# Carry matrices of a chunked recurrence built in one run of products, and two pairs of product loops interleaved

## The reference, cut to what matters

```
def step(S, inp):                      # S: 8 heads x 64 x 64, one step for each of 256 tokens
    r_t, w_t, k_t, v_t, kk_t, a_t = inp
    s_kk = einsum("bhvk,bhk->bhv", S, kk_t)
    S = S * w_t - s_kk[..., None] * (kk_t * a_t)[:, :, None, :] + v_t[..., None] * k_t[:, :, None, :]
    return S, einsum("bhvk,bhk->bhv", S, r_t)
```

## Time and profile before

| what | value |
|---|---|
| median of 3 runs | 1668.27 us (1666.89 to 1669.16) |
| profiled execution, its own time | 1668.85 us |
| its span | 1667.0 us |
| PE busy | 1591.9 us, 95% of the span |
| DVE, ACT, POOL busy | 1136.0, 838.3, 108.4 us |
| mean granted clock of PE | 0.98 of full speed |

### The profile page before, as it was taken

The page is one execution under the profiler, slowest core; times in us unless marked ns, Lnnn a source line. Parts: engine busy times, 40 slices in busy tenths (PEclk is TensorE's granted clock), DMA queues, the critical chain, the costliest instruction groups (busy, mean ns, idle before and its releaser), DMA issues.

```text
span 1667.0 us, 26114 instructions
## 1 busy us (share of the span) xinstructions
PE 1591.9 (95%) x10308; PEld 1388.3 (83%) x10308; DVE 1136.0 (68%) x1415; ACT 838.3 (50%) x1267; POOL 108.4 (7%) x145
## 2 busy tenths in 40 slices
PE   6888899989999999999899999999999999999999
PEld 6777789978888888887788888888889987788887
DVE  4775485558767777675767767766678956667675
ACT  6553255554444644454754444644457657654443
POOL 0258000000000000000000000000000015100000
PEclk9899899999999999999999999999999999999999
DMA  6230025335555454545335454555444541355553
GB/s 259 103 126 2 2 102 189 127 139 196 180 197 178 154 201 176 199 158 177 127 127 202 176 201 177 179 176 201 177 175 153 186 171 74 102 177 192 186 189 113
DMA packets 37075, 263.60 MB, mean 158 GB/s; under 512 B 4224, under 2 KB 4352, under 8 KB 5760
## 3 DMA queue, kind: packets, MB, share of 16 engines
q1 hardware_dynamic: 35712, 257.97, 43.5%
q0 software_dynamic: 704, 2.62, 0.4%
q10 hardware_dynamic: 576, 1.84, 0.3%
HBM read 261.36 MB, written 1.05 MB: 157 GB/s over the span
## 4 chain that ended last, share of the span: by engine, by line
PE 86%; DVE 8%; ACT 5%; issue 1%; DMA 1%; SPq 0%; DVEq 0%; ACTq 0%
PE PS L539 21%; PE PS L469 14%; PE PS L471 13%; PE PS L470 13%; PE PS L540 10%; PE PS L543 3%; PE PS L743 2%; PE PS L542 1%; DVE w_lo L1732 1%; ACT w_hi L1186 1%; PE PS L437 1%; DMA raw_weights<-W 1%; DVE arena L2032 1%; PE PS L553 1%; PE PS L757 1%
## 5 line engine op out<-in xcount | busy, mean ns | idle before, releaser
L1732 DVE TENSOR_TENSOR w_lo<-raw_weights,w_hi 128x1024 fp32r<-128x1024 f32 x488 | 592.9, 1232 | 367.5 <-ACT w_hi L1186 366.8
L1186 ACT ACTIVATE w_hi<-raw_weights 128x1024 fp32r<-128x1024 f32 x488 | 505.8, 1054 | 291.8 <-PE PS L471 141.4
L539 PE MATMUL PS<-h_both,w_hi 128*128 128x512 f32 x1470 | 527.5, 398 | 0.0
L540 PE MATMUL PS<-h_both,w_lo 128*128 128x256 f32 x1470 | 412.5, 281 | 0.0
L539 PEld LDWEIGHTS PS<-h_both,w_hi 128*128 128x128 f32 x1470 | 276.6, 188 | 59.0
L540 PEld LDWEIGHTS PS<-h_both,w_lo 128*128 128x128 f32 x1470 | 277.7, 189 | 8.7
L469 PE MATMUL PS<-h_both,w_hi 128*128 128x256 f32 x560 | 162.6, 290 | 10.1 <-DVE w_lo L1732 7.1
L469 PE MATMUL PS<-w_hi,g_hi 128*128 128x512 f32 x440 | 171.5, 390 | 0.0
L471 PE MATMUL PS<-w_hi,g_lo 128*128 128x512 f32 x440 | 171.2, 389 | 0.0
L470 PE MATMUL PS<-w_lo,g_hi 128*128 128x512 f32 x440 | 171.2, 389 | 0.0
L470 PE MATMUL PS<-h_both,w_hi 128*128 128x256 f32 x560 | 160.7, 287 | 0.0
(11 more groups left out here) (410 smaller groups left out, 1995.0 us busy)
## 6 DMA issues: line engine op xcount, KB each, us to landing
raw_weights<-W SPq DMA_DIRECT2D x244, 1024.0 KB, 4.8
post_gain<-post_gains POOLq DMA_DIRECT2D x3, 512.0 KB, 3.7
x_resid<-x SPq DMA_DIRECT2D x2, 512.0 KB, 6.9
arena<-mem POOLq DMA_DIRECT2D x1, 1024.0 KB, 5.3
out<-x_resid SPq DMA_DIRECT2D x2, 512.0 KB, 2.6
ptab<-cols ACTq DMA_DIRECT2D x1, 857.0 KB, 8.9
ctab<-consts ACTq DMA_DIRECT2D x1, 758.0 KB, 5.9
rtab<-rows ACTq DMA_DIRECT2D x1, 176.0 KB, 12.0
```

Source lines behind the costliest of these rows:

```text
L539: mm(both_out, hi, h_both[:, :, c, :], start=c == 0, stop=False)
L540: mm(PS[:, bank + j, 0:T], lo, h_hi[:, c, :], start=False, stop=False)
L1186: A(w_hi[:, n % H, :], raw[:, n % (2 * R), :], ACT.Copy).then_inc(S.hi_ready, 1)
L1732: v.tensor_tensor(w_lo[:, n % H, :], raw[:, n % (2 * R), :], w_hi[:, n % H, :].bitcast(F32), ALU.subtract).then_inc(S.lo_ready, 1)
```

## The change

`state_bu` and `rows_carried` take a list of chunks and alternate between them inside the loop over the four 128-column slices. `carry` becomes `carries`, which writes the identity of both carry matrices first, each as one product of 512 columns (the identity repeated four times by a broadcast view), and then the eight products of the two matrices in turn, chunk 1 (rows 64 to 127, bank 2) and chunk 2 (rows 0 to 63, bank 0). The calls move accordingly: chunk 1's `state_bu` goes ahead of the carries and is alternated with chunk 0's; chunk 2's carry moves ahead of `state_kv(1)` and `state_bu(2)`; PE waits for the second XA copy before both carries; `rows_carried(2)` waits for the last `z_ready` and alternates with `rows_carried(3)`. No instruction of another engine is changed.

```
-            def state_bu(g):
+            def state_bu(gs):
                 for c, cs in enumerate(pairs):
-                    last = mm(PS[:, 4 + g, cs], B_t[half(g), g // 2, cs], U0[half(g), g // 2, cs], start=False,
-                              stop=g == 0 and c == 3)
-                if g == 0:
-                    last.then_inc(S.z_done, 1)
+                    for g in gs:
+                        last = mm(PS[:, 4 + g, cs], B_t[half(g), g // 2, cs], U0[half(g), g // 2, cs], start=False,
+                                  stop=g == 0 and c == 3)
+                        if g == 0 and c == 3:
+                            last.then_inc(S.z_done, 1)
-            def carry(g, bank):
+            def carries():
+                banks = (2, 0)
+                for bank in banks:
+                    mm(PS[:, bank, :].rearrange("p (c d) -> p c d", c=4), ident_r,
+                       ident_r.unsqueeze(1).broadcast_to([P, 4, P]), start=True, stop=False)
                 for c, cs in enumerate(pairs):
-                    mm(PS[:, bank, cs], ident_r, ident_r, start=True, stop=False)
-                    last = mm(PS[:, bank, cs], XA[half(g), g // 2, cs], B_t[half(g), g // 2, cs], start=False, stop=True)
-                last.then_inc(S.gt_done, 1)
+                    for g, bank in zip((1, 2), banks):
+                        last = mm(PS[:, bank, cs], XA[half(g), g // 2, cs], B_t[half(g), g // 2, cs], start=False,
+                                  stop=c == 3)
+                        if c == 3:
+                            last.then_inc(S.gt_done, 1)
-            def rows_carried(g):
-                t, cp = g // 2, 64 * (g % 2)
+            def rows_carried(gs):
                 for c, cs in enumerate(pairs):
-                    last = mm(PS[cp:cp + 64, Y_BANK[g], cs], RT[...], Zs[g - 1][:, c, :], start=False, stop=c == 3)
-                last.then_inc(S.yc_done, 1)
+                    for g in gs:
+                        t, cp = g // 2, 64 * (g % 2)
+                        last = mm(PS[cp:cp + 64, Y_BANK[g], cs], RT[...], Zs[g - 1][:, c, :], start=False, stop=c == 3)
+                        if c == 3:
+                            last.then_inc(S.yc_done, 1)
             state_kv(0)
             ...
-            state_bu(0)
-            pe.wait_ge(S.xa_ready, 1)
-            carry(1, 2)
-            state_bu(1)
+            state_bu((0, 1))
+            pe.wait_ge(S.xa_ready, 2)
+            carries()
             pe.wait_ge(S.convY_ready, 4)
             state_kv(1)
             pe.wait_ge(S.u_ready, 2)
-            state_bu(2)
-            pe.wait_ge(S.xa_ready, 2)
-            carry(2, 0)
+            state_bu((2,))
             pe.wait_ge(S.gt_ready, 1)
             ...
             rows_own(1)
-            rows_carried(2)
             pe.wait_ge(S.z_ready, 3)
-            rows_carried(3)
+            rows_carried((2, 3))
```

More of the change, by code:

```diff
@@ L867, in rows_own @@
                                 last.then_inc(S.yc_done, 1)
-            def rows_carried(g):
-                t, cp = g // 2, 64 * (g % 2)
+            def rows_carried(gs):
                 for c, cs in enumerate(pairs):
-                    last = mm(PS[cp:cp + 64, Y_BANK[g], cs], RT[:, t * 512 + c * P + cp:t * 512 + c * P + cp + 64],
-                              Zs[g - 1][:, c, :], start=False, stop=c == 3)
-                last.then_inc(S.yc_done, 1)
+                    for g in gs:
+                        t, cp = g // 2, 64 * (g % 2)
+                        last = mm(PS[cp:cp + 64, Y_BANK[g], cs], RT[:, t * 512 + c * P + cp:t * 512 + c * P + cp + 64],
+                                  Zs[g - 1][:, c, :], start=False, stop=c == 3)
+                        if c == 3:
+                            last.then_inc(S.yc_done, 1)
             state_kv(0)
@@ L895, in _ @@
             pe.wait_ge(S.rt_ready, 1)
-            rows_carried(1)
+            rows_carried((1,))
             state_gz(2)
```

## The result

The changed kernel takes 1657.64 us (median of 4 runs, 1655.65 to 1659.30) against 1668.20 for the kernel before, run beside it: ratio 0.9935, 95% interval 0.9923 to 0.9948. That is 10.6 us faster (8.7 to 12.8 by the interval), where 8.2 to 8.7 were forecast (1660.0 against the median of the kernel before, 1660.1 against its profiled execution). The time lies inside the range of 1657 to 1666, 0.6 us above its lower end. The profiled execution took 1655.98 us, with a span of 1654.2.

What follows compares the result with a forecast made beforehand. PE's own work, in the order of products the change rewrites, was taken as the bound. Some 4.0 us from order and 4.7 from half clock sum to 8.7, giving 1660.0 us, range 1657.0 to 1666.0.

Steps and rivals of the forecast that it cites:

- 1. state_bu of chunks 0 and 1: Sixteen alternating instructions in place of eight take 0.98 us, the same as chunk 0's alone; chunk 1's own eight vanish.
- 2. wait for the second XA copy: PE's wait moves ahead of both carries; price 0, cover 2.0 us, at most 0.69 us were the copy late.
- 3. both carries: Two wide identities and one change of shape, 0.66 us, then sixteen alternating instructions, 1.00; sum 1.66, bounds 1.3 to 2.9.
- 4. state_kv(1), state_bu(2): Products behind the carries, chunk 2 alone in state_bu, all in one row half: 1.87 us, waits covered.
- 5. reads: 64 instructions of 64 x 64 in all four array quarters: 1.0 us at full clock, against 1.91 at half clock.
- 6. state_gz(1): Behind reads: 1.08 us at full clock like its twin state_gz(2), against 1.60 mostly at half clock.
- 7. rows_own, rows_carried(1), state_gz(2): Products behind state_gz(1), unchanged at 6.14 us; the moved z_ready wait keeps 0.8 us of cover.
- 8. last products to projection: Alternated rows_carried of chunks 2 and 3, then ACT evacuations: 2.39 us stays, price 0; without overlap 0.66 us lost.
- no fall of the clock: PE's clock stays at 1.00 throughout the stretch, with one-row-half products of 1.87 us left; chance 0.68.
- rival of the late evacuation: Pairing rows_carried of chunks 2 and 3 delays chunk 2's ACT evacuation by 0.66 us, to 1660.8; chance 0.04.
- the one of missing overlap: In carries the row halves don't overlap, or the repeated view is slow: 1.2 us more, 1661.3; chance 0.08.
- half clock of 4.7 us: Gain from full clock: 1.9 second carry, 1.3 the 2.72 us before it, 0.9 reads, 0.5 state_gz(1).

Runs made afterwards that it cites:

- run 7: Changed kernel with output products of chunks 2 and 3 one after the other, the last z_ready wait between them; median 1658.62 us, ratio 0.9940 to the kernel before.
- run 5: Changed kernel without alternating: state_bu and, behind both wide identities, carry products one chunk after the other; median 1662.23 us, ratio 0.9960 to the kernel before.
- run 3: Changed kernel with sliced carries again, a 128-column identity product ahead of each slice's product; median 1667.58 us, ratio 1.0002 to the kernel before.
- Run 4: Kernel before with one edit: each carry writes its identity as one 512-column product, order and halves as before; median 1659.12 us, ratio 0.9952.
- run 6: Changed kernel with each wide identity as four of 128 columns, all eight ahead of the carry products; median 1660.18 us, ratio 0.9951 to the kernel before.
- run 8: Changed kernel with 24 extra 64-row products, all in row half 0, just ahead of reads; median 1663.37 us, ratio 0.9967 to the kernel before.
- run 10: Changed kernel with eight extra pairs of a 128-row and a 64-row float32 product just ahead of reads; median 1664.18 us, ratio 0.9976 to the kernel before.

## Why the prediction was right

Step by step against the profile after, in us:

| step | forecast | measured |
|---|---|---|
| 1. state_bu of chunks 0 and 1 | 0.98 | 0.99 |
| 2. wait for the second XA copy | 0 | 0 |
| 3. both carries | 1.66 | 1.66 |
| 4. state_kv(1), state_bu(2) | 1.87 | 1.88 |
| 5. reads | 1.0 | 1.09 |
| 6. state_gz(1) | 1.08 | 1.09 |
| 7. rows_own, rows_carried(1), state_gz(2) | 6.14 | 6.14 |
| 8. last products to projection | 2.39 | 2.39 |
| whole stretch's gain | 8.7 | 8.59 |

Each duration was taken from a row of the kernel before in which the same shapes ran in the same pattern: `carries` was priced by state_kv(0), reads by L736 at full clock. That no fall of the clock would come was right too, and so were the waits that were to stay covered. The rival of the late evacuation is refuted by run 7, the one of missing overlap by run 5 and the table. The prediction named a rule of the Trainium skill ("TensorE: Matmul & The Clock Gate", The mechanism) that spoke for the late evacuation: a weight load overlaps products in flight only where the row group differs. This trace disagrees. The chunks of L882 share all 128 rows and differ in columns, and the sixteen products take 1.10 us alternated (1.59 in turn) with PE busy all through, while their weight loads take 0.86 of it:

```profile
207.22 0.86 PEld L882 LDWEIGHTS PS<-arena 128*64 128x64 f32 x16
```

Two things were off. The size: 10.6 and 10.0 us were measured, not 8.2 to 8.7, and the forecast time of 1660.0 lies 2.4 us above the median. The steps at full clock came out as forecast. The term that was too small is the half clock of 4.7 us, read from one profile in which it lasted 10.24 us; in the second profile of the same kernel it lasted 13.65, and the stretch was 27.39 us, 1.54 longer, a gain of 10.1 by the stretch. What lies outside the stretch moves from one execution to the next: it took 1636.9 to 1641.2 us in the fourteen profiles, 1641.2 and 1639.3 before and 1636.9 and 1640.3 after. So nothing shows that the 4.3 us by which the first two profiles differ outside the stretch belong to the change, and that the first median came so near the low end of the range was partly chance. The detail: the idle time before L469 was said to stay at 0.80 us, although the same text had PE done 0.4 us earlier; it is 1.29.

The reason given for the clock was only half right. Order decides it: the fall is there in both profiles of the kernel before and in run 3, and in none of the eleven profiles without sliced carries. The mean clock of the whole span, which is on record for most executions, agrees: it is 0.984 or less in 46 of the 68 with sliced carries, and in none of the 59 without. Run 4 takes nothing but the slices away and the clock holds; run 6 has as many identity and product instructions as run 3, in another order, and holds too. But with 7.2 us of products in one row half, which the prediction named as well, the clock did not fall (run 8), and with changes of shape between float32 products alone it did not either (run 10). What is left is the mixture itself, gone through four times for one carry: a one-instruction identity product, a change, a 64-row product, a change, three instructions in 0.67 us. So the prediction was right that the clock would hold, and lucky in part of its reason: it had counted step 4, products in one row half, as what was left of the danger. Which part of the mixture matters, the kind of identity product, its operands or the changes beside it, was not tried, and stays open.

## What to carry to other kernels

Price a new order of products by a stretch of the old trace where the same shapes already run in that pattern; here that was good to 0.1 us in eight steps. Group short products by shape, and write a constant that many slices need as one wide product: the 128-column identities between other products cost 1.2 us a carry directly, and through the clock, for two carries, 3.1 us in run 3 and an estimated 4.7 in the first profile of the kernel before, behind the place where they stand. Where a gain hangs on a stretch of half clock, look at more than one profile: its length differed by a third between two executions of one kernel.

## What the runs showed of the hardware

- The granted clock fell to 1.2 GHz while PE was busy without a gap: 2.7 and 3.6 us after the start of the first sliced carry in the second and the first profile of the kernel before (0.1 and 1.0 behind its end), and 6.1 us after it in run 3 (0.8 behind the end of both). It stayed low for 13.65, 10.24 and 6.83 us.
- Two 64-row products in different row halves cost together what one costs, 0.11 us a step; 48 instructions in one half and 96 alternated both took 5.3 us. Two 128-row products in different column halves overlap as well: sixteen instructions took 1.10 us alternated and 1.59 in turn, and their weight loads ran beneath them.
- Products at the seam of two calls in different row halves overlap without being alternated: sixteen instructions of state_bu, one chunk after the other, took 1.54 us, not the 1.78 of sixteen steps of 0.111.
